# Two gated feed-forwards on Trainium2: multiply by the token's inverse root after the first projection instead of before it

## The reference

```python
def rmsnorm(x, g):
    y = x * lax.rsqrt(jnp.mean(x * x, axis=-1, keepdims=True) + EPS)
    return y * g

def conv_glu_ffn(h, w_in, conv_w, conv_b, w_out):      # FFN_DIM = 2752
    u = h @ w_in                                       # 1024 -> 2 * 2752
    up = jnp.pad(u, ((0, 0), (CONV_WIDTH - 1, 0), (0, 0)))
    c = conv_b
    for tap in range(CONV_WIDTH):                      # 3 taps along the tokens
        c = c + up[:, tap:tap + S] * conv_w[tap]
    return (jax.nn.silu(c[..., :FFN_DIM]) * c[..., FFN_DIM:]) @ w_out

# layer l:
x = x + attention(rmsnorm(x, attn_norm_g[l]))
x = x + conv_glu_ffn(rmsnorm(x, ffn_norm_g[l]), ffn_w_in[l], ...)
```

## Time and profile before

| | us |
|---|---|
| median of 3 runs | 670.37 (669.89 to 672.5) |
| the profiled execution | 669.92 |
| its span, first to last instruction | 668.1 |
| TensorE (PE) busy | 639.7 (96%) |
| VectorE (DVE) busy | 511.7 (77%) |
| ScalarE (ACT) busy | 415.9 (62%) |
| mean granted TensorE clock | 0.994 |

### The profile page before, as it was taken

How to read it: one execution, slowest core, us unless ns; L and a number is a source line. 1 busy time by engine, 2 the same in 40 slices (tenths; PEclk the granted TensorE clock), 3 DMA queues, 4 the chain that set the end, 5 groups by cost and what they waited for, 6 DMA issues and landing times.

```text
span 668.1 us, 11022 instructions
## 1 busy us (share of the span) xinstructions
PE 639.7 (96%) x3662; PEld 537.2 (80%) x3662; DVE 511.7 (77%) x990; ACT 415.9 (62%) x856; POOL 19.1 (3%) x69
## 2 busy tenths in 40 slices
PE   7999989999999999999999999979999999999994
PEld 7998666578888888888887788768888888888893
DVE  4587578955888888888877547786888888888886
ACT  6554367836766666666657454663966666666655
POOL 2100000000000000000002000050000000000000
PEclk9999999999999999999999999989999999999998
DMA  7685020126355555555533545306355555555511
GB/s 277 236 288 200 10 118 2 64 69 248 122 200 195 199 194 196 175 222 200 189 110 130 186 155 183 119 1 219 130 192 191 192 196 196 197 198 197 197 72 65
DMA packets 21443, 109.02 MB, mean 163 GB/s; under 512 B 2593, under 2 KB 2977, under 8 KB 12449
## 3 DMA queue, kind: packets, MB, share of 16 engines
q1 hardware_dynamic: 21120, 108.36, 45.4%
q10 hardware_dynamic: 288, 0.22, 0.1%
HBM read 107.52 MB, written 1.05 MB: 162 GB/s over the span
## 4 chain that ended last, share of the span: by engine, by line
PE 82%; DVE 10%; ACT 5%; issue 2%; POOL 1%; DMA 0%; DVEq 0%; ACTq 0%
PE psA L397 13%; PE psA L398 13%; PE psA L399 13%; PE psO L504 10%; PE psT L504 10%; PE psO L509 5%; PE psT L509 5%; DVE stat L1657 2%; DVE win_lo L1369 1%; DVE arena L1686 1%; PE psO L695 1%; ACT win_hi L1023 1%; PE psO L883 1%; PE psT L680 1%; ACT arena L982 1%
## 5 line engine op out<-in xcount | busy, mean ns | idle before, releaser
L1471 DVE TENSOR_TENSOR win_lo<-stage,win_hi 128x1024 fp32r<-128x1024 f32 x90 | 109.6, 1219 | 5.7 <-ACT win_hi L1023 5.7
L1488 DVE SCALAR_TENSOR_TENSOR arena<-arena,prm 128x255 f32<-128x255 f32 (+1 forms) x152 | 73.5, 484 | 50.8 <-ACT arena L1049 48.0
L1023 ACT ACTIVATE win_hi<-stage 128x1024 fp32r<-128x1024 f32 x92 | 96.0, 1051 | 7.8 <-PE psA L399 5.6
L504 PE MATMUL psO<-hA,win_hi 128*128 128x512 f32 x304 | 95.5, 395 | 0.0
L504 PE MATMUL psT<-hA,win_hi 128*128 128x512 f32 x304 | 95.1, 394 | 0.0
L1369 DVE TENSOR_TENSOR win_lo<-stage,win_hi 128x1024 fp32r<-128x1024 f32 (+3 forms) x58 | 65.1, 1161 | 24.7 <-ACT win_hi L959 24.4
L1049 ACT ACTIVATE arena<-arena,prm 128x256 f32<-128x256 f32 x76 | 45.8, 602 | 58.3 <-DVE arena L1494 58.1
L397 PE MATMUL psA<-wout_hi,act_hi 128*128 128x512 f32 x176 | 69.0, 392 | 0.2
L959 ACT ACTIVATE win_hi<-stage 128x1024 fp32r<-128x1024 f32 (+3 forms) x56 | 53.5, 1003 | 24.7 <-PE psA L399 16.9
L398 PE MATMUL psA<-wout_lo,act_hi 128*128 128x512 f32 x176 | 68.7, 390 | 0.0
L399 PE MATMUL psA<-wout_hi,act_lo 128*128 128x512 f32 x176 | 68.5, 389 | 0.0
(11 more groups left out here) (293 smaller groups left out, 1216.6 us busy)
## 6 DMA issues: line engine op xcount, KB each, us to landing
stage<-in_w_ffn_in SPq DMA_DIRECT2D x44, 1024.0 KB, 5.4
stage_out<-in_w_ffn_out SPq DMA_DIRECT2D x44, 516.0 KB, 3.5
stage<-in_w_kv SPq DMA_DIRECT2D x8, 1024.0 KB, 4.8
stage<-in_w_group SPq DMA_DIRECT2D x5, 1024.0 KB, 5.3
stage<-in_w_nsa_out SPq DMA_DIRECT2D x4, 1024.0 KB, 5.1
stage<-in_w_dq SPq DMA_DIRECT2D x4, 1024.0 KB, 4.8
stage<-in_w_dout SPq DMA_DIRECT2D x4, 1024.0 KB, 4.8
stage<-in_w_phi SPq DMA_DIRECT2D x2, 1024.0 KB, 4.8
```

The source lines that it names most:

```text
L504: mm(o, win_hi[:, slot, cs], hA[:, k, :, :].rearrange("p a q -> p (a q)"), start=k == 0, stop=False)
L1023: act.activation(win_hi[:, slot, h * W // 2:(h + 1) * W // 2], stage[:, slot, h * W // 2:(h + 1) * W // 2], ACT.Copy).then_inc(sem["in_hi" ...
L1471: last = dve.tensor_tensor(win_lo[:, slot, cs], stage[:, slot, cs], win_hi[:, slot, cs].bitcast(F32), sub)
L1488: dve.scalar_tensor_tensor(conv[:, b, g, k:S], src[:, 0:S - k], prm[:, b, 4 * g + 2 - k:4 * g + 3 - k], conv[:, b, g, k:S], ALU.mult, ALU. ...
```

## The change

The inverse root of a token is a factor of its whole row of x, so it is also a factor of its column of u, which has tokens along the free axis. The changed kernel transposes x without its norm, with only the gains applied, and multiplies u by a row of the 256 inverse roots.

- TensorE: tile 0's eight transposes (`raw_T`) are issued inside the out-projection, four ahead of each of its last two groups of three matmuls. Tile 1's first four follow it, the other four stand behind the first two k tiles of `up_raw`, which takes the place of up(0), goes into banks 0 and 1 of `psA`, and takes the k tiles in the order `T_ORDER`. `stay_warm` and `xsT` are gone. `row_T` transposes a broadcast of `rstd` into a row on all partitions; `up_second` is up(1) with a wait after each half of its weights.
- ScalarE: squares, roots and high parts interleaved by hand; the scaling of x is gone. In a step `u_part` is one copy of both halves, and `split_in(j+2, b, 0)` stands ahead of both first taps.
- VectorE: `raw_lo`, the mean, `split_out(0, 0)` and the Newton steps of both tiles at once, interleaved; the row is copied to SBUF; every chunk's u is multiplied by it (`times_row`, or in `add_and_scale` in place, on 512 elements). The two additions become one. `split_in(j+2, b, 0)` stands ahead of the taps.
- The last steps multiply u by the row from PSUM, `product_lo` and first taps change places, and in layer 0 `split_in(NJ, 0, 0)` is later on both engines. A split of the following projection (`split(C_KV, (1,))`) stands behind the additions at the end of layer 0's feed-forward.
- `psT` and `psO` become views of one PSUM tensor `psU`, so that one instruction can read both halves of a chunk.

```diff
+T_ORDER = (0, 2, 1, 3, 4, 6, 5, 7)
...
-        psT = ctx.enter_context(nc.psum_tensor("psT", [P, 2, 512], F32))
-        psO = ctx.enter_context(nc.psum_tensor("psO", [P, 2, 512], F32))
+        psU = ctx.enter_context(nc.psum_tensor("psU", [P, 2, 2, 512], F32))
+        psT, psO = psU[:, :, 0, :], psU[:, :, 1, :]
...
+        row_src = arena[:, 5120:5376].rearrange("p (t q) -> p t q", t=TT)
+        row = arena[:, 5376:5632]
...
+            def raw_T(n, t, half):
+                pe_.wait_ge(sem["x_new"], 2 * TT * X_NEW[n] + 2 * t + half + 1)
+                xT_part(x, t, range(half * KT // 2, (half + 1) * KT // 2))
...
                     for n in range(2):
+                        if kk == KT - 1 and t == TT - 1:
+                            raw_T(n_norm, 0, n)
...
+                def up_raw(h_waits, n):
+                    raw_T(n, 1, 0)
+                    slot = first % 2
+                    pe_.wait_ge(sem["in_hi"], 2 * (first + 1))
+                    pe_.wait_ge(sem["in_lo"], first + 1)
+                    for i, k in enumerate(T_ORDER):
+                        if i == 2:
+                            raw_T(n, 1, 1)
+                        pe_.wait_ge(sem["xT_hi"], h_waits + i + 1)
+                        pe_.wait_ge(sem["xT_lo"], h_waits + i + 1)
+                        for g in range(2):
+                            cs = slice(k * 2 * P + g * P, k * 2 * P + g * P + P)
+                            last = three_w(psA[:, g, 0:S], slot, cs, k, i == 0, i == KT - 1)
+                    last.then_inc(sem["in_used"], 1)
+                def row_T():
+                    pe_.wait_ge(sem["row_src"], layer + 1)
+                    for t in range(TT):
+                        last = pe_.transpose(psA[:, 2, t * P:(t + 1) * P], row_src[:, t, :], ident[:, :])
+                    last.then_inc(sem["row_bank"], 1)
...
-                up(0, 0, KT * (1 if layer == 0 else 4), halves=False)
-                up(1, 1)
-
+                up_raw(KT * (1 if layer == 0 else 4), 1 if layer == 0 else 3)
+                row_T()
+                up_second()
                 down(0, 0, True, False)
...
# ScalarE, in a step
+                    act.wait_ge(sem["in_used"], j + (first + 1))
+                    if halves:
+                        act.activation(u_part, psU[:, b, :, S:2 * S], ACT.Copy).then_inc(sem["u_part"], 1)
+                        split_in(j + 2, b, 0)
+                    act.wait_ge(sem["u_norm"], j + (f0 + layer + 1))
                     for g in range(2):
+                        conv_first(j, b, g, u_sum[:, g, :])
...
# ScalarE, entry
-                normalise()
-                h_hi(hA_hi, O_FG + layer * KT, 1 if layer == 0 else 3)
+                act.activation(warm, eps, ACT.Sqrt)
+                square_halves(n, 0)
+                root_of(n, 0)
+                raw_hi(layer, inst, waits, 0)
+                raw_hi(layer, inst, waits, 2)
+                square_halves(n, 1)
+                raw_hi(layer, inst, waits, 4)
+                root_of(n, 1)
+                raw_hi(layer, inst, waits, 6)
...
# VectorE, in a step
+                def add_parts(j, b):
+                    dve.wait_ge(sem["u_part"], j + layer * (NJ - 3))
+                    dve.tensor_tensor(u_sum, psU[:, b, :, 0:S], u_part, ALU.add).then_inc(sem["u_sum"], 1)
+                def add_and_scale(j, b):
+                    add_parts(j, b)
                     take_params(j + 1, 1 - b)
+                    dve.wait_ge(sem["u_sum"], j + layer * (NJ - 3))
+                    dve.tensor_tensor(u_sum, u_sum, rows, ALU.mult).then_inc(sem["u_norm"], 1)
...
+                def step(j, b):
+                    add_and_scale(j, b)
+                    split_in(j + 2, b, 0)
+                    taps(j, b)
+                    product(j, b)
+                    split_in(j + 2, b, 1)
+                    product_lo(j, b)
+                    split_out(j + 1, 1 - b)
...
# VectorE, entry (behind the additions)
+                raw_lo(0)
+                raw_lo(1)
+                raw_lo(2)
+                raw_lo(3)
+                first_mean(n, 1)
                 take_params(0, 0)
+                split_out(0, 0)
+                raw_lo(4)
+                newton_a()
+                raw_lo(5)
+                newton_b()
+                raw_lo(6)
+                newton_c()
+                raw_lo(7)
+                newton_d()
+                rows_of_rstd()
                 split_in(1, 1, 0)
+                dve.wait_ge(sem["row_bank"], layer + 1)
+                dve.tensor_copy(row, psA[:, 2, 0:S]).then_inc(sem["row_ready"], 1)
+                dve.wait_ge(sem["row_ready"], layer + 1)
+                times_row(0, psA[:, 0:2, 0:S])
                 split_in(1, 1, 1)
+                take_params(1, 1)
+                taps(0, 0)
+                product(0, 0)
+                split_in(2, 0, 0)
+                product_lo(0, 0)
+                split_in(2, 0, 1)
+                split_out(1, 1)
                 step(1, 1)
```

More of the change, by code:

```diff
@@ L1012, in x_new, with ffn @@
                 return f
-            def ffn(layer, first, normalise):
+            def ffn(layer, first, n):
                 f0 = layer * NJ
@@ L1097, in last_steps @@
                     if layer == 0:
+                        split_in(NJ, 0, 0)
                         split_in(NJ, 0, 1)
@@ L1473, in split_in, with raw_lo @@
                         last.then_inc(sem["in_lo"], 1)
+                    elif isinstance(j, int) and j == 1:
+                        last.then_inc(sem["half_lo"], 1)
+                def raw_lo(i0):
+                    for k in T_ORDER[i0:i0 + 1]:
+                        n_hi[0] += 1
+                        dve.wait_ge(sem["xT_hi"], n_hi[0])
+                        dve.scalar_tensor_tensor(hA_lo[:, k, :], free_banks[k // 2][:, (k % 2) * S:(k % 2 + 1) * S], gain(O_FG + layer * KT, k),
+                                                 hA_hi[:, k, :].bitcast(F32), ALU.mult, sub).then_inc(sem["xT_lo"], 1)
                 def split_out(j, b):
@@ L1525, in last_steps @@
[L1525 to L1532 removed]
+                    taps(j, 0)
@@ L1768, in _ @@
                     add_y(2, t, h, "out_used", NJ)
+            split(C_KV, (1,))
             h_lo(hA_lo, hA_hi, O_KG)
```

280 lines of the change are left out of this document (126 added, 154 removed).

## The result

The changed kernel took 668.25 us in the median of ten runs (665.56 to 669.17), the kernel before 671.25 us in ten runs beside it (669.76 to 672.53). The ratio is 0.9941, with a 95% interval of 0.9925 to 0.9957: 4.0 us less, 3.0 to 5.0. The prediction was 665.1 us on a median then shown as 670.37, a gain of 5.3 us; it lies outside the interval by 0.3 us, the measured time lies inside the predicted range. The profiled execution took 667.75 us, with a span of 666.0.

A forecast was written before the change was run, and what follows sets the result against it. TensorE's matmul count was taken to bound the loop, the norm's chain to delay each entry. Two entries at 2.65 take 5.3 us off the span, 668.1 to 662.8; with 1.8 around the span and 0.45 to the median, 665.1; range 661.5 to 668.8.

The forecast's parts named there:

- Transposes inside the out-projection: End of out-projection: each group of four costs 0.36 us to the next matmul, which runs 0.08 longer; 2 x 0.44.
- First matmul of `up_raw`: Feed-forward entry, layer 0: starts at 164.1 and not 168.15, after tile 1's first transposes and the two splits.
- Row's transposes: Entry, between `up_raw` and the second `up`: two transposes on TensorE, 0.22 us.
- `down(0)`: Entry, layer 0: starts at 176.9 after waiting 0.7, instead of 179.79.
- `down(1)`: Step 1, layer 0: starts at 185.6, where it was 188.25; gain 2.65 us per layer.
- past 165: Entry, layer 0: the prediction is wrong if the first matmul of `up_raw` waits past 165.
- no hole ahead of the taps: Loop, VectorE: ScalarE's taps run under the split, both holes go (1.26); step 7.5 us, under TensorE's 8.3.
- Taken as nothing; at worst 0.3 per layer: Last steps, three multiplies of 0.34 each: `down(21)` stays at 346.07, because the last `wout_lo` still waits for `down(19)`.
- Rival 1: Entries: unseen operations and a dozen hand-overs cost more, 1.65 later; 1.0 gained per layer, 668.4; chance 0.14.
- The unseen operations: Entry, chain over the row: three operations without rows, at their upper bound 0.15 more each.
- Rival 2: Loop: VectorE becomes the bound, holes stay, step 8.72, 0.43 over TensorE's; 681; chance 0.08.
- Rival 3: Entry: clock falls to 1.2 GHz in `up_raw`, 5.8 more per layer; 677; chance 0.05.

The follow-up runs named there:

- experiments 2 and 3: Changed kernel with the loop's multiply by the row done twice: 670.35 us, ratio 0.9986; changed kernel without the loop's multiply: 667.65 us, ratio 0.9939.
- experiment 9: Changed kernel with GpSimd making chunk 1's low `down` weights, step 0's low product before VectorE's split, GpSimd's result awaited only before step 1's `split_out`: 670.82 us, ratio 0.9986.
- Experiment 6: Changed kernel with the tail's add and multiply of the gate's half waiting only for that half's 24 matmuls, not the whole up: 665.49 us, ratio 0.9920.
- experiment 12: The changed kernel run again, unaltered, against the kernel before: 666.88 us, ratio 0.9946.
- experiment 1: Changed kernel with the loop's old order on VectorE, half by half with the split behind the taps, ScalarE's waits following: 700.24 us, ratio 1.0426.
- experiment 4: Kernel before with its twenty matmuls for warmth between out-projection and transposes left out: 672.65 us, ratio 1.0040.

## Why the prediction came out as it did

**The direction and the mechanism were right.** The gain is in the two entries and nothing is gained or lost in the loop (experiments 2 and 3).

**The entry, step by step** (the prediction's times with the 2.02 of lateness added). Transposes inside the out-projection 0.36 and 0.08: 0.35 and 0.09. First matmul of `up_raw` 166.12: 166.29. Its length with four transposes 6.26: 6.31. Row's transposes 0.22: 0.35 to the next matmul. `down(0)` 178.92 after a wait of 0.7: 179.25 after 0.49. `down(1)` 187.62: 187.90. The clock 1.00: 1.00. Per layer 2.65 was predicted and 2.37 to 2.4 measured, 0.25 to 0.28 less. Both `down`s start behind `act_lo` (178.78 and 187.42, 0.42 long each), so VectorE's chain from the copy of the row on sets them:

```profile
173.02 0.42 DVE L1641 COPY arena<-psA 128x256 f32<-128x256 f32 x1 [0.21 <-PE psA L504]
...
178.78 0.42 DVE L1544 TENSOR_TENSOR act_lo<-arena,act_hi 128x256 fp32r<-128x256 f32 x1
```

The copy was to be at 172.82 and is 0.20 late, since it waits for the row's transposes: 0.17 comes from the first hand-over, where ScalarE and VectorE take 0.96 us behind the last transposes, and 0.05 from `up_raw`. The multiply follows at 173.47, 0.45 behind the copy and not 0.4. The 0.35 at the row is not on this path, for TensorE has 0.49 to spare ahead of `down(0)`. Nor is it the price of two transposes: `up_second` starts at 172.95, 0.15 behind the end of VectorE's half split (171.57 to 172.80), which it needs, and in experiment 9 `up(2)` starts 0.14 behind the split that held it. The profile names no releaser here, so that this is the cause is not shown.

The prediction also named as a sign of being wrong a first matmul of `up_raw` "past 165". The raw mark, 166.29, is past it; without the 2.02 by which this execution was late it is 164.27. An absolute time is a poor sign in a kernel whose executions differ by that much ahead of the change.

**The loop.** The step was to be 7.5 us with no hole ahead of the taps. It can be read from step 1, which finds its `up` done. VectorE in the changed kernel, against the earlier trace rows:

```profile
181.38 0.68 DVE L1519 TENSOR_TENSOR arena<-psU,arena 128x512 f32<-128x512 f32 x1
...
182.10 0.69 DVE L1526 TENSOR_TENSOR arena<-arena 128x512 f32<-128x512 f32 x1
182.71 1.22 DVE L1479 TENSOR_TENSOR win_lo<-stage,win_hi 128x1024 fp32r<-128x1024 f32 x1
183.85 1.91 DVE L1505 SCALAR_TENSOR_TENSOR arena<-arena,prm 128x255 f32<-128x255 f32 x4
...
188.89 0.68 DVE L1519 TENSOR_TENSOR arena<-psU,arena 128x512 f32<-128x512 f32 x1
```

It is 7.51 us, from 181.38 to 188.89, and the four taps follow the split at once. The multiply is 0.61 to the next start, where 0.60 was taken from bounds of 0.57 and 0.75.

**The ends were mis-sized.** "Taken as nothing; at worst 0.3 per layer" is the step that failed. From `down(1)` on, 0.44 was lost in layer 0 and 0.6 in layer 1; 0.32 of each is the tail's (0.22 held at `down(21)` and 0.10 behind it). The prediction followed the product of step 21, rightly 0.7 later (343.86 and not 343.20), and stopped at its partner, the last `wout_lo`, which "still waits for `down(19)`". Before, it did. ScalarE and VectorE in the kernel before:

```profile
343.61 1.16 ACT L1094 ACTIVATE wout_hi<-stage_out 128x512 fp32r<-128x512 f32 x2 [0.71 <-PE psA L399]
344.27 1.29 DVE L1550 TENSOR_TENSOR wout_lo<-stage_out,wout_hi 128x512 fp32r<-128x512 f32 x2 [0.65 <-ACT wout_hi L1094]
```

And in the changed kernel:

```profile
343.41 0.42 ACT L1103 ACTIVATE arena<-arena 64x256 f32<-64x256 f32 x1 [1.07 <-DVE arena L1598]
...
344.39 1.29 DVE L1609 TENSOR_TENSOR wout_lo<-stage_out,wout_hi 128x512 fp32r<-128x512 f32 x2
```

Now ScalarE's copy no longer waits for TensorE: it follows at 343.73 behind its own silu (343.41), which waits for VectorE's tap. So VectorE's chain sets the time: two multiplies (0.76), a wait of 0.35 for ScalarE's tap, and one more multiply between the product and the low product (0.42) are in one row up to `act_lo` at 345.60. Experiment 6 takes 0.31 of it away by letting one multiply start earlier.

**The sum.** 5.3 predicted. Less 0.25 to 0.28 in two entries, less 0.44 and 0.6 at the ends, plus the 0.4 that the second attention took less: 4.1, against 4.0 (3.0 to 5.0) measured. That 0.4 belongs to no term of the prediction, and executions of one code differ by as much there; without it the change is worth 3.7 us, and part of the nearness of 5.3 to 4.0 is luck. Rival 1 (2.0 gained) is not ruled out by the medians, which differ by 3.0 here and by 4.5 in experiment 12, but by the marks: its reason would leave 1.0 per entry, and they show 2.37 to 2.4. The unseen operations cost about what they were taken for. Rival 2 would have been real without the new order (experiment 1). Rival 3 didn't occur in the changed kernel; experiment 4 may make it more serious than its 0.05, for the kernel before.

**The best version.** Experiment 6, at 0.9920 (0.9898 to 0.9943), beats the kernel before; its interval overlaps that of the changed kernel, whose tail it shortens by 0.31 and 0.37 us in its two layers in the profile.

## What to carry to other kernels

Work added to an engine that is not the bound is free only in its order: here 26 us of multiplies cost nothing where a long independent operation lies over the other engine's latency, and 32 us where it doesn't. Follow an added operation to the ends of a loop as well as through its middle, since the first and the last steps have no slack. Before a wait is taken out by moving an operation forward, look at what the wait was hiding, and before work is moved to GpSimd, count the time for which it would keep VectorE from SBUF.

## What the runs showed of the hardware

VectorE and GpSimd shut each other out where both read two operands from SBUF: a VectorE split of 1.22 us took 3.43 beside a GpSimd operation of 2.83.

A 128x128 float transpose took TensorE 0.11 us whether it stood among matmuls (0.44 for a group of four) or among its own kind (0.88 for eight more in a row).

The first 512-column matmul behind a wait of TensorE was followed by the next 0.34 us later (`down(0)` at 179.25, `down(21)` at 346.06), where matmuls of its kind follow each other at 0.23: such a wait cost 0.1 us beyond its own length.

The runs of one kernel spread over 3 to 4 us, and a good part of it is the granted clock in one stretch of the first layer's attention: 1.00 in some executions, in others down to 0.5, the lower of TensorE's two levels (1.2 and 2.4 GHz), for some 3 to 6 us. TensorE was busy throughout 88 to 92 us in all of them, those that fell and those that didn't. The marks behind it lie up to 3.8 us apart (163.81 to 167.59 for the first matmul of `up_raw`), the opening's own spread of up to 0.9 us within it, in kernels that are the same up to there. A change of 2 us per layer is read from distances inside one profile, not from its absolute times.
